# HGRN2 recurrence: value projections computed for two tiles at once, in 512-column products, with the sixteen weight tiles in another order

## The chip, the cores and the metric

The kernel runs on one core of one Trainium2 chip. The metric is the device time of one launch in microseconds. Three runs of the kernel before gave a median of 2646.62 us.

## The reference, cut to what matters

The program is two transformer blocks and a third one with a gated linear recurrence (HGRN2), all on 512 tokens of width 1024, in float32. The change is inside the recurrence stage of the last block. Its input projection gives four tensors, `q`, `f`, `i` (the values, called `v` in the kernel) and `g`:

```python
def _hgrn2_mixer(h, w_in, lower_bound, out_norm, w_out):
    proj = h @ w_in                                  # (512,1024) @ (1024,4096)
    q, f, i, g = jnp.split(proj, 4, axis=-1)
    ...                                              # log_f and k from f, qf = silu(q)/sqrt(128)
    o = _hgrn2_chunk_scan(heads(qf), heads(k), heads(i), heads(log_f))   # 8 heads of 128
    o = o * lax.rsqrt(jnp.mean(o * o, axis=-1, keepdims=True) + NORM_EPS)
    o = o.reshape(b, s, D_MODEL) * out_norm * jax.nn.silu(g)
    return o @ w_out
# S_t = diag(f_t) S_{t-1} + k_t v_t^T ;  o_t = S_t^T q_t
```

## The kernel before

Each float32 product is made of three matmuls on a high and a low part of either operand (hi x hi, hi x lo, lo x hi). The 4096 columns of `hgrn_w_in_2` are taken in sixteen tiles of 1024 x 256, named by tensor and pair of heads: ("f", 0) is the f tile of heads 0 and 1. `HG_TILES` is their order. A tile passes through one of two slots, by its place in the list (even places slot 0, odd places slot 1): SyncE's queue loads it into `w_raw` once the tile two places ahead of it has been split; ScalarE makes `w_hi_t` in two halves (`conv`, line 910) after the last matmul on the tile that held the slot; VectorE makes `w_lo_t` in four quarters (`rest`, line 1207; GpSimd does this in other stages).

A tile is used in two units, and a unit in two fills of one half each (`("gemm", u, h)`). For f, q and g a fill is 12 matmuls with a weight block as the stationary operand and 512 tokens moving (`unit_part`, lines 1785, 1786, 1790). For v the tokens are stationary, 128 at a time, and 256 weight columns move, so that a fill is 24 matmuls (`v_part`, lines 1800 to 1802). ScalarE takes a unit out of its PSUM bank (`unit_out`): two sigmoids for f (lines 850, 851), silu for q and g (853, 858), a scaled copy for v (855) into `hg_v`, which holds one pair of heads.

The order of all steps is written out by `hgrn_sequence`, which every engine walks and from which it picks its own steps. For each pair of heads j = 0..3 there are twelve slots: ten levels of the scan (`lev`: TensorE multiplies keys by queries, VectorE then multiplies Q and K by decay factors, lines 1176 and 1177, in `update`, and keeps the scores in `hg_p`, in `keep`) and two outputs (`out`, line 1723). After the TensorE part of a slot come one or two fills of the projection, which cover VectorE's update for the next level. `after(k, step)` places a step behind the k-th next fill: `prep` (VectorE finishes f and k of a unit, lines 1214 and 1215), `rest`, `far`, and the output norm of the pair before (`hn`, lines 1229 and 1231, and `lo`, line 1236). The order of fills before is v0 f1 q1 g0 in pair 0, v1 f2 q2 g1 in pair 1, v2 f3 q3 g2 in pair 2, v3 g3 in pair 3, with f0 and q0 ahead of the loop; with `HG_FILLS` each of slots 0 to 6 has one fill, slots 7 to 10 have two and slot 11 has one.

VectorE walks its steps in order: a `prep` that waits for ScalarE's sigmoid holds back the `lev` behind it. TensorE waits for `hg_qk` (VectorE's updates) at each level, and for `w_hi` and `w_rest` before the hi and the lo products of a fill on a new tile.

## Time and profile before

| | value |
|---|---|
| median of 3 runs | 2646.62 us |
| lowest, highest | 2646.04, 2647.33 us |
| the profiled execution's own time | 2649.84 us |
| its span in the profile | 2648.0 us |
| TensorE busy | 2593.1 us, 98% of the span |
| granted TensorE clock, mean | 0.992 |
| recurrence, from its first level (1982.56) to the first whole unit of the output projection (2257.70) | 275.1 us |

The profile's clock starts at the first instruction. Starts of matmuls are recorded and their ends are modelled, so a matmul's shown duration is longer than the distance to the next one; distances between starts are what counts. A granted clock of 1.00 is 2.4 GHz, 0.50 is 1.2 GHz, and a value between them is a mean over a stretch that has both.

### The profile page before, as it was taken

What the parts mean: (1) busy time and instruction counts of PE and PEld (TensorE: products, weight loads), DVE (VectorE), ACT (ScalarE), POOL (GpSimd) and SP (SyncE); (2) the same over time, 40 slices, a digit from 0 to 9 for tenths busy, and PEclk for the clock granted to TensorE, in tenths of its full rate; (3) what the DMA queues carried; (4) which work ended last, traced back from release to release, by engine and by line L of the source; (5) the groups of instructions that cost most, each with busy time, mean ns of one, the idle gap of its engine ahead of it and who ended that gap; (6) DMA issues with size and microseconds to landing.
All of it is one profiled execution on the core that took longest, in us unless ns stands there. A gap on an engine that the chain in (4) does not pass through costs nothing.

```text
span 2648.0 us, 30661 instructions
## 1 busy us (share of the span) xinstructions
PE 2593.1 (98%) x12780; PEld 2155.9 (81%) x12780; DVE 1092.8 (41%) x1563; ACT 890.0 (34%) x1361; POOL 1000.3 (38%) x404
## 2 busy tenths in 40 slices
PE   6999999999999999999999999999999999999998
PEld 5788888776888888788888988888888888888887
DVE  5635254454532225844345254211164555512213
ACT  4222225565422223422224333222252333423322
POOL 1445444221454544444444434444430000444442
PEclk8999999999999999999999999999999999999999
DMA  6555344211333343455452324233232221232331
GB/s 242 202 183 199 119 155 130 67 56 48 112 127 127 127 135 124 163 167 183 135 187 88 109 80 163 92 101 100 89 96 64 64 64 49 90 102 96 96 96 64
DMA packets 249088, 310.56 MB, mean 117 GB/s; under 512 B 7356, under 2 KB 228301, under 8 KB 248950
## 3 DMA queue, kind: packets, MB, share of 16 engines
q1 hardware_dynamic: 245962, 304.94, 34.9%
q10 hardware_dynamic: 2988, 3.66, 0.4%
q8 instruction: 101, 1.65, 0.3%
q14 instruction: 37, 0.30, 0.0%
HBM read 306.46 MB, written 4.74 MB: 118 GB/s over the span
## 4 chain that ended last, share of the span: by engine, by line
PE 93%; DVE 3%; DMA 1%; issue 1%; ACT 1%; POOL 0%; SPq 0%; DVEq 0%; ACTq 0%
PE bank L1773 20%; PE bank L1768 20%; PE bank L1769 20%; PE bank L1785 5%; PE bank L1786 5%; PE bank L1790 5%; PE bank L1751 2%; PE bank L1696 2%; PE bank L1752 2%; PE bank L1753 2%; PE bank L1800 1%; PE bank L1801 1%; PE bank L1802 1%; PE bank L1613 1%; PE bank L1633 1%
## 5 line engine op out<-in xcount | busy, mean ns | idle before, releaser
L757 POOL TENSOR_TENSOR w_lo_t<-w_raw,w_hi_t 128x1024 fp32r<-128x1024 f32 (+1 forms) x400 | 1000.1, 2520 | 1617.2 <-ACT w_hi_t L910 1617.0
L910 ACT CAST w_hi_t<-w_raw 128x1024 fp32r<-128x1024 f32 (+1 forms) x432 | 424.9, 1032 | 688.2 <-PE bank L1773 582.6
L1768 PE MATMUL bank<-h_hi,w_hi_t 128*128 128x512 f32 x1648 | 644.4, 391 | 5.2 <-issue 2.7
L1769 PE MATMUL bank<-h_lo,w_hi_t 128*128 128x512 f32 x1648 | 643.2, 390 | 0.0
L1773 PE MATMUL bank<-h_hi,w_lo_t 128*128 128x512 f32 x1648 | 415.2, 391 | 0.0
L1768 PEld LDWEIGHTS bank<-h_hi,w_hi_t 128*128 128x128 f32 x1648 | 310.6, 188 | 71.1 <-issue 3.6
L1769 PEld LDWEIGHTS bank<-h_lo,w_hi_t 128*128 128x128 f32 x1648 | 310.6, 188 | 64.4 <-issue 0.2
L1773 PEld LDWEIGHTS bank<-h_hi,w_lo_t 128*128 128x128 f32 x1648 | 309.3, 188 | 63.9
L1323 DVE SCALAR_TENSOR_TENSOR scr<-scr,cact 128x1024 f32<-128x1024 f32 x112 | 257.7, 2301 | 89.4 <-DMA scr<-in_ada_w 81.2
L1768 PE MATMUL bank<-act_hi,w_hi_t 128*128 128x512 f32 x720 | 280.3, 389 | 1.3 <-ACT w_hi_t L910 1.2
L1769 PE MATMUL bank<-act_lo,w_hi_t 128*128 128x512 f32 x720 | 280.1, 389 | 0.0
L1471 DVE TENSOR_TENSOR bank<-hidden,bank 128x512 f32<-128x512 f32 x88 | 60.9, 694 | 442.1 <-ACT hidden L1050 442.1
L1494 DVE SCALAR_TENSOR_TENSOR x<-bank,half,x 128x512 f32<-128x512 f32 x88 | 66.1, 751 | 338.1 <-PE bank L1773 260.9
L1773 PE MATMUL bank<-act_hi,w_lo_t 128*128 128x512 f32 x720 | 179.0, 389 | 0.4 <-POOL w_lo_t L757 0.4
L1050 ACT ACTIVATE hidden<-bank 128x512 f32<-128x512 f32 x88 | 52.6, 598 | 369.1 <-PE bank L1773 369.1
L1768 PEld LDWEIGHTS bank<-act_hi,w_hi_t 128*128 128x128 f32 x720 | 135.2, 188 | 30.1 <-issue 1.6
L1773 PEld LDWEIGHTS bank<-act_hi,w_lo_t 128*128 128x128 f32 x720 | 135.0, 188 | 29.2 <-POOL w_lo_t L757 1.3
L1769 PEld LDWEIGHTS bank<-act_lo,w_hi_t 128*128 128x128 f32 x720 | 135.2, 188 | 28.0
L1785 PE MATMUL bank<-act_hi,w_hi_t 128*128 128x512 f32 x320 | 129.0, 403 | 3.1 <-DVE act_lo L1147 3.0
L1786 PE MATMUL bank<-act_lo,w_hi_t 128*128 128x512 f32 x320 | 125.4, 392 | 0.0
L1785 PE MATMUL bank<-h_hi,w_hi_t 128*128 128x512 f32 x288 | 121.3, 421 | 0.0
L1790 PE MATMUL bank<-act_hi,w_lo_t 128*128 128x512 f32 x320 | 114.7, 391 | 0.0
(251 smaller groups left out, 3377.4 us busy)
## 6 DMA issues: line engine op xcount, KB each, us to landing
scr<-in_ada_w SPq DMA_DIRECT2D x128, 512.0 KB, 6.8
w_raw<-in_ffn_wg SPq DMA_DIRECT2D x44, 1024.0 KB, 5.3
w_raw<-in_ffn_wu SPq DMA_DIRECT2D x44, 1024.0 KB, 5.4
w_raw<-in_ffn_wd SPq DMA_DIRECT2D x32, 1024.0 KB, 5.3
w_raw<-in_mlp_w SPq DMA_DIRECT2D x32, 1024.0 KB, 5.4
w_raw<-in_hgrn_w_in SPq DMA_DIRECT2D x16, 1024.0 KB, 5.6
w_raw<-in_ffn_wd SPq DMA_DIRECT2D x16, 768.0 KB, 4.7
w_raw<-in_attn_w_qkv SPq DMA_DIRECT2D x12, 1024.0 KB, 5.1
```

Source lines behind the costliest of these rows:

```text
L757: nc.gpsimd.tensor_tensor(w_lo_t[:, t % 2, k], w_raw[:, t % 2, k], w_hi_t[:, t % 2, k].bitcast(F32), ALU.subtract).then_inc(w_lo, 1)
L910: act.copy(w_hi_t[:, slot, k], w_raw[:, slot, k]).then_inc(w_hi, 1)
L1323: dve.scalar_tensor_tensor(acc, src, cact[:, kb:kb + 1], acc, ALU.mult, ALU.add).then_inc(ada_ch, 1)
L1471: dve.tensor_tensor(ps[2 + b][:], blk(hidden, 4 + (2 * i + b) % 4), ps[2 + b][:], ALU.mult).then_inc(v_done, 1)
L1494: ins_ = dve.scalar_tensor_tensor(xb, acc[:], gate_col(op, nb), xb, ALU.mult, ALU.add)
L1696: mm = pe.matmul(ps[2 + s % 2][:, n * 64:(n + 1) * 64], K[:, tok], late, start=True, stop=True)
L1768: pe.matmul(dst, w, blk(m_hi, kb), start=kb == 0, stop=False)
L1769: pe.matmul(dst, w, blk(m_lo, kb), start=False, stop=False)
L1773: last = pe.matmul(dst, w_lo_t[:, slot, kb, b * P:(b + 1) * P], blk(m_hi, kb), start=False, stop=kb == kbs - 1)
L1785: pe.matmul(dst, w, blk(m_hi, kb), start=kb == 0, stop=False)
L1786: pe.matmul(dst, w, blk(m_lo, kb), start=False, stop=False)
L1790: last = pe.matmul(dst, w_lo_t[:, slot, kb, b * P:(b + 1) * P], blk(m_hi, kb), start=False, stop=kb == kbs - 1)
```

## The change

The value tiles are taken in pairs. v0 and v1 are neighbours in the new order (places 2 and 3), v2 and v3 too (places 10 and 11), so that each pair fills both weight slots. A value unit is now one block of 128 tokens for both tiles: its matmuls move 512 weight columns, 256 from each slot, and a fill is 12 matmuls (`v_wide`) where it was 24. `hg_v` has four buffers, and ScalarE's copy is two instructions of 256 columns. Both slots are held until the last unit of the pair, so the `conv` steps of both following tiles stand behind it, one after the other. The order of fills is now v0 v1 f1 q1 | g0 f2 q2 g1 | v2 v3 f3 q3 | g2 g3, in the same slots and counts. The `rest` steps around a value pair, and `hn` and `lo` after pairs 0 and 2, get other places.

```diff
--- before.py
+++ after.py
@@ -267,18 +267,24 @@
 
 
 
-HG_TILES = [("f", 0), ("q", 0), ("v", 0), ("f", 1), ("q", 1), ("g", 0), ("v", 1), ("f", 2), ("q", 2), ("g", 1),
-            ("v", 2), ("f", 3), ("q", 3), ("g", 2), ("v", 3), ("g", 3)]
+HG_TILES = [("f", 0), ("q", 0), ("v", 0), ("v", 1), ("f", 1), ("q", 1), ("g", 0), ("f", 2), ("q", 2), ("g", 1),
+            ("v", 2), ("v", 3), ("f", 3), ("q", 3), ("g", 2), ("g", 3)]
 HG_COL = {"g": 3 * D, "v": 2 * D, "f": D, "q": 0}
 HG_FILLS = (1, 1, 1, 1, 1, 1, 1, 2, 2, 2, 2, 1)
 HG_WO_EARLY = 6
 HG_RESTS = 16
 HG_REST_AT = (2, 3, 3, 4)
+HG_REST_TWO = ((2, 2, 3, 3), (3, 4, 4, 5))
 
 
 def hg_unit(kind, j, b):
 
     return 2 * HG_TILES.index((kind, j)) + b
+
+
+def hg_v_block(u):
+
+    return u - hg_unit("v", HG_TILES[u // 2][1] // 2 * 2, 0)
 
 SG_MIX = {3: (0,), 4: (1, 2), 5: (3, 4), 6: (5, 6), 7: (7,)}
 
@@ -293,9 +299,18 @@
 
     def flush_convs():
         seq.extend(convs)
-        for _, i in convs:
+        for n, (_, i) in enumerate(convs):
             if i < HG_RESTS:
-                for q, k in enumerate(HG_REST_AT):
+                if len(convs) == 2:
+                    places = HG_REST_TWO[n]
+                elif HG_TILES[(i + 2) % 16] in (("v", 1), ("v", 3)):
+                    places = (0, 0, 1, 1)
+                else:
+                    places = HG_REST_AT if i else (1, 2, 2, 3)
+                for q, k in enumerate(places):
+                    if k == 0:
+                        seq.append(("rest", i, q))
+                        continue
                     after(k, ("rest", i, q))
         del convs[:]
 
@@ -303,7 +318,10 @@
         kind, j = HG_TILES[u // 2]
         if kind == "f":
             after(1, ("prep", j, u % 2))
-        if u % 2:
+        if kind == "v":
+            if hg_v_block(u) == TB - 1:
+                convs.extend([("conv", u // 2 - 1), ("conv", u // 2)])
+        elif u % 2:
             convs.append(("conv", u // 2))
 
     def fill(*step):
@@ -348,8 +366,9 @@
                 if j < 3:
                     seq.append(("osum", j))
                     for b in range(2):
-                        after(2 + b, ("hn", j, b))
-                        after(3 + b, ("lo", j, b))
+                        k = 2 + b if j % 2 else 3 + 2 * b
+                        after(k, ("hn", j, b))
+                        after(k + 1, ("lo", j, b))
     fill("wo", 1, 0, 0, HG_WO_EARLY)
     seq.append(("osum", 3))
     fill("wo", 1, 1, 0, HG_WO_EARLY)
@@ -450,7 +469,7 @@
         sg_b = vec[:, V_SG + 8:V_SG + 16]
         sg_wn = hidden[:, 0:1024].rearrange("p (g t) -> p g t", g=8)
         sg_mask = hidden[:, 1024:1152]
-        hg_v = scr[:, 0:1024].rearrange("p (t n) -> p t n", t=TB)
+        hg_v = [scr[:, c:c + 1024].rearrange("p (t n) -> p t n", t=TB) for c in (0, 8640, 9664, 10688)]
         hg_g = scr[:, 1024:2048].rearrange("p (h t) -> p h t", h=2)
         hg_f = scr[:, 2048:4096].rearrange("p (b t) -> p b t", b=2)
         hg_k = scr[:, 4096:6144].rearrange("p (b t) -> p b t", b=2)
@@ -842,8 +861,6 @@
                 act.wait_ge(blk_mm, 2 * op.t0 + u + 1)
                 if kind in "fq" and j >= 2:
                     act.wait_ge(hg_mm, 10 * (j - 1))
-                if kind == "v" and j:
-                    act.wait_ge(o_mm, 8 + 2 * j)
                 if kind == "g" and j:
                     act.wait_ge(o_ok, 8 + 2 * j)
                 if kind == "f":
@@ -852,8 +869,9 @@
                 elif kind == "q":
                     act.activation(hg_q[:, j % 2, cols], bank[:], ACT.Silu).then_inc(hg_ev, 1)
                 elif kind == "v":
-                    act.activation(hg_v[:, 2 * b:2 * b + 2, :], bank[:].rearrange("p (t n) -> p t n", t=2), ACT.Copy,
-                                   scale=H_SCALE).then_inc(hg_ev, 1)
+                    tb, j0 = hg_v_block(u), j // 2 * 2
+                    act.activation(hg_v[j0][:, tb, :], bank[:, 0:TW], ACT.Copy, scale=H_SCALE)
+                    act.activation(hg_v[j0 + 1][:, tb, :], bank[:, TW:2 * TW], ACT.Copy, scale=H_SCALE).then_inc(hg_ev, 1)
                 else:
                     act.activation(hg_g[:, b, :], bank[:], ACT.Silu).then_inc(hg_ev, 1)
 
@@ -1650,7 +1668,7 @@
                     pe.wait_ge(a_lo_s, op.a0 + k1)
                     unit_part(ps[2 * s + b][:], s, b, a_hi_t, a_lo_t, k0, k1, KB)
 
-        def hgrn_pe(pe, op, npre, first, unit_part, v_part, w_half):
+        def hgrn_pe(pe, op, npre, first, unit_part, v_wide, w_half):
             for step in hgrn_sequence():
                 if step[0] == "first":
                     w_half(op.t0, 0)
@@ -1665,9 +1683,8 @@
                             pe.wait_ge(pre_root, npre)
                     bank = ps[u if u < 4 else u % 2]
                     if HG_TILES[u // 2][0] == "v":
-                        if u % 2 == h == 0:
-                            w_half(t, 0)
-                        mm = v_part(bank[:, h * TW:(h + 1) * TW], t % 2, 2 * (u % 2) + h, t if u % 2 == h == 0 else None)
+                        tb = hg_v_block(u)
+                        mm = v_wide(bank[:].rearrange("p (j n) -> p j n", j=2), tb, 4 * h, 4 * h + 4, None if tb else t)
                     else:
                         mm = unit_part(bank[:], t % 2, u % 2, h_hi, h_lo, 4 * h, 4 * h + 4, KB,
                                        t if u % 2 == 0 else None)
@@ -1716,11 +1733,11 @@
                     if b == 0:
                         pe.wait_ge(hg_pc, 9 * (j + 1))
                         pe.wait_ge(hg_far, 3 * j + 3)
-                        pe.wait_ge(hg_ev, hg_unit("v", j, 1) + 1)
+                        pe.wait_ge(hg_ev, hg_unit("v", j | 1, 1) + 1)
                     if j:
                         pe.wait_ge(o_ok, 8 + 2 * (j - 1) + b + 1)
                     for c in range(TB):
-                        mm = pe.matmul(ps[6 - b][:, c * P:S], hg_v[:, c, b * P:(b + 1) * P],
+                        mm = pe.matmul(ps[6 - b][:, c * P:S], hg_v[j][:, c, b * P:(b + 1) * P],
                                        hg_p[:, (b * TB + c) * S:(b * TB + c) * S + S - c * P],
                                        start=c == 0, stop=c == TB - 1)
                     mm.then_inc(o_mm, 1)
@@ -1800,6 +1817,20 @@
                     pe.matmul(dst, h_hi[:, tok], w_hi_t[:, slot, kb, :], start=kb == 0, stop=False)
                     pe.matmul(dst, h_hi[:, tok], w_lo_t[:, slot, kb, :], start=False, stop=False)
                     last = pe.matmul(dst, h_lo[:, tok], w_hi_t[:, slot, kb, :], start=False, stop=kb == KB - 1)
+                return last
+
+            def v_wide(dst, tb, k0, k1, tile):
+
+                toks = [slice(kb * S + tb * P, kb * S + (tb + 1) * P) for kb in range(KB)]
+                if tile is not None:
+                    pe.wait_ge(w_hi, 2 * tile + 2 + k1 // 4)
+                for kb in range(k0, k1):
+                    pe.matmul(dst, h_hi[:, toks[kb]], w_hi_t[:, :, kb, :], start=kb == 0, stop=False)
+                    pe.matmul(dst, h_lo[:, toks[kb]], w_hi_t[:, :, kb, :], start=False, stop=False)
+                if tile is not None:
+                    w_half(tile + 1, k1 // 4 - 1)
+                for kb in range(k0, k1):
+                    last = pe.matmul(dst, h_hi[:, toks[kb]], w_lo_t[:, :, kb, :], start=False, stop=kb == KB - 1)
                 return last
 
             def nat_unit(slot, half_, banks, tile=None):
@@ -2064,7 +2095,7 @@
                                                    sg_v[:, c, g * P:(g + 1) * P], sg_ws[:, g, :], start=True, stop=True)
                                 mm.then_inc(sg_mm, 1)
                 elif op.kind == "hgrn":
-                    hgrn_pe(pe, op, npre, lambda: first_units(op, 0, norm, npre - 1), unit_part, v_part, w_half)
+                    hgrn_pe(pe, op, npre, lambda: first_units(op, 0, norm, npre - 1), unit_part, v_wide, w_half)
 
 INPUTS = [
     "x", "c", "rel_bias", "ada_w", "ada_b", "ln_ffn1", "ffn1_wg", "ffn1_wu", "ffn1_wd", "ln_mix", "ln_ffn2",
```

## Rows read from the trace of the kernel before

**Rows 1.** The page: the span, and the busy time of each engine

```profile
span 2648.0 us, 30661 instructions
PE 2593.1 (98%) x12780; PEld 2155.9 (81%) x12780; DVE 1092.8 (41%) x1563; ACT 890.0 (34%) x1361; POOL 1000.3 (38%) x404
```

**Rows 2.** TensorE's waits, 1982 to 2258: total us, times, longest

```profile
PE bank L1702 <- DVE scr L1177: 1.9, 3, 0.6
PE bank L1696 <- DVE scr L1177: 1.2, 3, 0.4
PE bank L1686 <- ACT scr L853: 0.8, 1, 0.8
```

**Rows 3.** The chain in the recurrence: start us, us, what

```profile
1987.45 1.74 PE bank L1696 x16
...
2001.43 1.73 PE bank L1696 x16
...
2015.06 1.73 PE bank L1696 x16
...
2022.97 1.16 PE bank L1702 x8
...
2065.45 2.00 PE bank L1696 x16
```

**Rows 4.** TensorE's timeline, second to last matmul of a value fill

```profile
1984.54 0.28 PE L1801 MATMUL bank<-w_lo_t,h_hi 128*128 128x256 f32 x1
...
1987.17 0.28 PE L1802 MATMUL bank<-w_hi_t,h_lo 128*128 128x256 f32 x1
```

**Rows 5.** The chain, units of 24 matmuls of 512 columns

```profile
2298.67 1.81 PE bank L1773 x8
...
2325.87 1.81 PE bank L1773 x8
```

**Rows 6.** VectorE's timeline, pair 1, between levels 2 and 3

```profile
2060.91 1.29 DVE L1207 TENSOR_TENSOR w_lo_t<-w_raw,w_hi_t 128x512 fp32r<-128x512 f32 x2
...
2062.72 0.75 DVE L1229 SCALAR_TENSOR_TENSOR sq<-bank,vec,ssq 128x512 f32<-128x512 f32 x1
...
2064.72 0.68 DVE L1177 TENSOR_TENSOR scr<-scr 128x512 f32<-128x512 f32 x1
```

**Rows 7.** ScalarE's timeline at three places

```profile
1965.51 0.37 ACT L965 CAST h_hi<-bank 128x256 fp32r<-128x256 f32 x1 [0.48 <-DVE bank L1298]
1965.78 1.05 ACT L910 CAST w_hi_t<-w_raw 128x1024 fp32r<-128x1024 f32 x1
...
2001.47 0.60 ACT L855 ACTIVATE scr<-bank 128x512 f32<-128x512 f32 x1 [8.72 <-PE bank L1802]
2001.96 1.98 ACT L910 CAST w_hi_t<-w_raw 128x1024 fp32r<-128x1024 f32 x2
...
2019.65 0.60 ACT L850 ACTIVATE scr<-bank 128x512 f32<-128x512 f32 x1 [8.02 <-PE bank L1790]
```

**Rows 8.** The page's DMA issues: count, KB each, us to landing

```profile
w_raw<-in_hgrn_w_in SPq DMA_DIRECT2D x16, 1024.0 KB, 5.6
```

**Rows 9.** TensorE's timeline: the first matmul after a pause, pause in brackets

```profile
444.10 1.10 PE L1602 MATMUL bank<-sq,blk 128*128 128x512 f32 x2 [1.53 <-ACT scr L951]
...
637.63 0.80 PE L1785 MATMUL bank<-act_hi,w_hi_t 128*128 128x512 f32 x1 [3.05 <-DVE act_lo L1147]
...
1117.26 0.50 PE L1768 MATMUL bank<-h_hi,w_hi_t 128*128 128x512 f32 x1 [2.08 <-DVE bank L1471]
...
2635.56 0.70 PE L1826 MATMUL bank<-ssq,ones 128*128 128x256 f32 x2 [1.97 <-DVE ssq L1273]
```

**Rows 10.** Windows: us, busy PE, PEld, DVE, ACT, POOL, PEclk, DMA, GB/s

```profile
442.00:450.00 8.00, 6.47 (x26) 4.59 (x25) 1.50 (x2) 5.02 (x7) 2.40 (x2) 1.00 0.00 0
636.00:644.00 8.00, 6.37 (x18) 4.47 (x19) 3.22 (x13) 2.40 (x9) 0.00 (x0) 0.57 0.04 15
1116.00:1124.00 8.00, 6.75 (x22) 5.37 (x23) 7.72 (x8) 3.07 (x4) 4.56 (x2) 0.79 0.42 146
```

## The prediction

> **What bounds the kernel now.** I read the page first: TensorE is busy 2593.1 of 2648.0 us [rows 1], so time comes only from what TensorE issues or waits for; VectorE at 41% and ScalarE at 34% matter where TensorE waits for them. In the recurrence TensorE's waits add up to 1.9 + 1.2 + 0.8 = 3.9 us in seven pauses [rows 2]. Everything else there is matmuls one behind the other. So the change can give back two things, a shorter value projection and part of 3.9 us, and it can add pauses. A pause costs a little more than it shows, since a 512-column matmul is shown 0.39 us long but the next starts 0.23 us after it: 0.16 us more each.
>
> I then read the chain to price a slot. With a value fill in it, three slots take 2001.43 - 1987.45 = 13.98 us, 4.66 each; with an f fill, three take 2015.06 - 2001.43 = 13.63, 4.54 each [rows 3]. The level's own matmuls are the same in both.
>
> **Term 1, the value products.** There are 16 value fills before and 16 after, all in slots with one fill but the last of each new pair. Before, each has 24 matmuls of 256 columns; after, 12 of 512, which is what an f fill issues. The price of one goes from 4.66 to 4.54, 0.12 us less, so 16 x 0.12 = 1.9 us less. Two bounds. From the distances inside a fill, 22 steps take 1987.17 - 1984.54 = 2.63 us, 0.1195 each [rows 4], and in units of 512 columns five units of 24 take 27.20 us, 0.2267 each [rows 5]: 24 x 0.1195 = 2.87 against 12 x 0.2267 = 2.72, 0.15 a fill and 2.4 us in all. The other bound is 0, if moving two stretches of 256 from two slots costs a restart; I take no such cost, as the f fills too read blocks from different places. I take -1.9, with ends -2.4 and 0.
>
> What fixed part of a matmul is saved can be seen from the same rows: 256 columns at 2.4 GHz are 106.7 ns of the 119.5, and 512 are 213.3 of the 226.7, so about 13 ns of each matmul don't go with its columns, and 192 of these go away. The Trainium skill ("TensorE: Matmul & The Clock Gate", section "Back-to-back issue gap") has the distance as N/2.4 plus 2.5 ns; by that rule the 192 matmuls would give back 0.5 us, and the sum below would be +2.1 instead of +0.7. The rows differ from it, and I go by the rows.
>
> **Term 2, VectorE's late update in pairs 1, 2 and 3.** Three of the pauses are at level 3 of these pairs, 1.2 us in all, 0.4 each [rows 2]. What is late is VectorE's update: between level 2 and the update it does two rests (1.29), `lo`, two `hn` operations, and the second update operation begins at 2064.72 and ends at 2065.40 [rows 6]; TensorE starts at 2065.45 [rows 3]. In pairs 1 and 3 the `lo` is moved behind, and the two rests stay: 0.69 us sooner. TensorE, with three cheaper fills ahead, comes 3 x 0.12 = 0.36 sooner, so a pause of 0.41 becomes about 0.1. In pair 2 the two rests are moved ahead of level 1, but `lo` then waits for ScalarE's copy, which stands behind the value unit's evacuation; I get about the same 0.1. So 3 x 0.3 = 0.9 us less, plus the 0.16 behind each pause where it goes away altogether: I take -1.1, with ends 0 and 3 x 0.57 = -1.7. The steps that are moved later in pairs 1 and 3 (`hn` of the second head at level 4, `lo` at level 5) find VectorE with slack: a slot is 4.54 us and its work there is update 1.3, small products and `keep` about 1.2, norm 1.4. The four quarters of tile 3 that now stand ahead of level 1 in pair 0 end about 0.1 us before that update is wanted; I count 0.
>
> **Term 3, the hand-over after a value pair.** This is the new wait. Before, a tile's `w_hi` was made while TensorE worked on the tile in the other slot. After, both slots are in use up to the last matmul of the pair, and the fill that follows at once, without a level between (slot 7 has two fills), is f1 (or f3) on a tile that isn't converted. Where a value unit ended before a conversion, the last matmul's modelled end was 2001.43 [rows 3], the evacuation started at 2001.47, and the conversion 0.49 later at 2001.96; its first half takes 1.05 [rows 7]. Now the evacuation is two instructions of 256 columns; such an instruction starts the next one 0.27 us later (1965.51 to 1965.78, [rows 7]). So w_hi's first half is there at 0.04 + 2 x 0.27 + 1.05 = 1.63 us after the modelled end, TensorE starts 0.05 later, a pause of 1.68, and with 0.16 the slot loses 1.84. There are two pairs: +3.7 us. Ends: 1.74 each if two copies cost what the one did, 3.5; 2.3 each if they cost 0.49 each and something over, 4.6.
>
> The low part is no further wait: the fill has eight hi products first (8 x 0.2267 = 1.8 us), and VectorE, idle since its update and `keep` of level 7, needs 0.05 and two rests (1.29 us, [rows 6]) from the first half on. The second half of `w_hi` and its rests come a microsecond behind that, ahead of the next fill. Behind the pause on TensorE stand levels 8 and 9, whose updates aren't late. On ScalarE four conversion halves (about 4 us) now stand in one row, and end before the next unit is out. On SyncE's queue the load of g0 (place 6) waits for the rests of f1, some 12 us later than before; it lands in 5.6 us [rows 8], about 6 us before its conversion is due. The load of f2 has more room. No load is added.
>
> **Term 4, `prep`.** Three pauses of 0.64 are at level 8 [rows 2]: sigmoid from 2019.65 [rows 7], then prep, update, level at 2022.97 [rows 3], 3.3 us for what one fill of 2.7 covers. In pairs 0 and 2 the tile f1 or f3 is now one tile later, so this `prep` leaves level 8 and the first `prep` comes ahead of level 9, again with one fill to cover the same chain. The pause goes with it: 0, with ends -1.6 (it vanishes twice) and +1.0 (the rests in front delay it by half a microsecond each).
>
> **The sum.** -1.9 - 1.1 + 3.7 + 0 = +0.7 us. The profiled execution's own time was 2649.84 us (span 2648.0 and 1.8 around it), 3.2 above the median of the runs. I put the sum on the median: 2646.6 + 0.7 = 2647.3 us; the profiled execution would be 2650.5.
>
> **The rivals.**
>
> *Each pause takes the clock down.* The new pauses are longer than any in the recurrence. Elsewhere a pause of 1.53 us was followed by a stretch at 1.00, and pauses of 1.97, 2.08 and 3.05 by falls: 0.79 over the 8 us from 1116, 0.57 over the 8 us from 636 [rows 9, 10]. Mine are about 1.7, between. At 0.79 the 8 us lose 1.7 us, so one fall gives 2649.0 and both give 2650.7, still within 0.2%. The Trainium skill ("TensorE: Matmul & The Clock Gate", section "A second HAM failure mode: psum-queue depth-cycling") warns that small idle times between groups of matmuls make the clock swing; in this trace the seven short pauses of the recurrence didn't, since its clock reads 1.00.
>
> *Slower, outside 0.2%.* The same mechanism at the price of the longest pause: 8 x 0.43 = 3.4 us for each pair, +0.7 + 6.9 = 7.6, 2654.2 us. It decides from two falls of 2.3 us each, that is when TensorE runs at 1.2 GHz for 4.6 us and more after each pause. [...]
>
> *Faster.* The pair's end is cheap (the conversion is quicker than I think), `prep` is covered at level 9, and the fills give the whole 2.4: -2.4 - 1.7 - 1.6 + 3.5 = -2.2, 2644.4. For more than 0.2% both hand-overs would have to be free as well, -5.7.
>
> *It does nothing.* The v fills stay at 4.66 and VectorE stays late: +3.7, 2650.3; still no change that can be told.
>
> **How the numbers follow.** About 0.2% (5.3 us) is what a measurement of this kernel can tell from no change. Sum as forecast, no clock fall: 0.45. One or both pauses with a fall of 1.7 us: 0.32. Nothing gained from the fills or the updates: 0.05. Small gain as in the third rival: 0.10. Dear clock falls or an unseen wait, over 5.3 us: 0.06. Everything covered: 0.02. The range reaches from the small gain, 2644.4, to both falls with some of the ends of term 3, 2651.5. Within 0.2%: 0.45 + 0.32 + 0.05 + 0.10 = 0.92; slower 0.06; faster 0.02.
>
> **What the profile after would show.** Value groups of 128 columns by 512 with 64 instructions for each of three lines, and slots of 4.54 us (term 1; wrong if 4.6 and more). No wait of a level on VectorE over 0.2 us at level 3 (term 2). Two new pauses of TensorE of 1.6 to 1.8 us, put down to ScalarE's conversion (term 3; wrong if rests or loads are named, or if they are much over 2). Pauses of 0.64 at level 9 in pairs 0 and 2, at level 8 in pair 1 only (term 4). A granted clock of 1.00 behind the new pauses; where it is 0.5 for some 3 us, the first rival holds. The forecast fails if the pauses are covered by something that I read as serial, or if a slot after the pair waits again.

## The result, and the profile after

| | before | after |
|---|---|---|
| median, us | 2646.45 (20 runs) | 2651.24 (20 runs) |
| lowest to highest | 2644.27 to 2648.85 | 2647.52 to 2655.03 |
| ratio, with 95% interval | | 1.0020 [1.0014, 1.0026] |
| span of the profiled execution | 2648.0 | 2648.6 |
| recurrence, first level to first whole unit of the output projection | 275.14 | 278.35 |
| from there to the end of the span | 390.3 | 392.5 |

The change made the kernel 4.8 us slower, just inside the 5.3 us that I had called no change; I had forecast 2647.3, 0.7 slower. TensorE issues 12588 matmuls where it issued 12780, so the products were made wide as written. First come TensorE's waits in the recurrence (total us, times, longest), to be held against [rows 2]:

```profile
PE bank L1802 <- ACT w_hi_t L928: 3.5, 2, 1.8
PE bank L1713 <- DVE hidden L1209: 1.3, 2, 1.0
PE bank L1728 <- DVE scr L1195: 1.3, 2, 0.6
PE bank L1703 <- ACT scr L870: 0.8, 1, 0.8
PE bank L1719 <- DVE scr L1195: 0.6, 1, 0.6
```

They are 7.5 us where they were 3.9. The first line is the hand-over after a value pair, which I had forecast (two pauses of 1.8). The second I had not: level 1 (line 1713) waits for VectorE's `keep` (line 1209), 1.0 us in pair 0 and 0.3 in pair 2. Level 3's three pauses of 0.4 are no longer among the waits. The `prep` chain now waits at level 9 twice (1728) and at level 8 once (1719). The chain (start us, us, what) of pair 0 shows the second line at work:

```profile
1978.59 0.97 DVE w_lo_t L1225 x2
1979.56 0.24 issue
1979.80 1.29 DVE w_lo_t L1225 x2
1981.09 1.14 DVE scr L1184
1982.22 1.21 DVE hidden L1209 x2
1983.43 0.14 issue
1983.57 1.97 PE bank L1713 x16
...
1988.36 1.73 PE bank L1713 x16
...
2011.06 1.73 PE bank L1713 x16
...
2020.39 0.89 PE bank L1719 x8
...
2027.37 1.99 PE bank L1728 x8
```

The four quarters of tile v1's split, the update for level 1, and the two parts of `keep` stand one behind the other on VectorE, and level 1 begins when the last is done. From 1988.36 to 2011.06 are five slots of 4.54 us, where value slots took 4.66 [rows 3]. And from level 7 (2011.06) to level 8 (2020.39) are 9.3 us, before 7.9 [rows 3]: the hand-over, against the `prep` pause that has moved to 2027.37. ScalarE's timeline of the hand-over, and TensorE's, to be held against [rows 7]:

```profile
2015.65 0.38 ACT L873 ACTIVATE scr<-bank 128x256 f32<-128x256 f32 x1 [8.45 <-PE bank L1833]
2015.93 0.38 ACT L874 ACTIVATE scr<-bank 128x256 f32<-128x256 f32 x1
2016.20 2.94 ACT L928 CAST w_hi_t<-w_raw 128x1024 fp32r<-128x1024 f32 x3
```

```profile
2017.39 0.47 PE L1802 MATMUL bank<-h_hi,w_hi_t 128*128 128x512 f32 x1 [1.77 <-ACT w_hi_t L928]
```

There are two copies 0.28 apart, then a conversion, for whose first half TensorE waits. The windows of 8 us behind the two pauses, to be held against [rows 10]:

```profile
2016.00:2024.00 8.00, 6.61 (x33) 5.65 (x34) 3.10 (x5) 5.37 (x7) 0.00 (x0) 1.00 0.36 107
2155.00:2163.00 8.00, 6.63 (x33) 5.67 (x34) 3.10 (x5) 5.35 (x7) 0.00 (x0) 1.00 0.39 108
```

The granted clock stayed at 1.00. All this makes +3.2 us for the recurrence. The rest is at the end of the program. These are its last 12 us, in the view of the DMA queues (packets, MB, share of 16 engines):

```profile
q1 hardware_dynamic: 576, 2.10, 43.9%
q8 instruction: 1, 0.02, 1.0%
issues: line engine op xcount, KB each, median us to landing
out<-scr SPq DMA_DIRECT2D x4, 512.0 KB, 5.1
```

In the kernel before, the same view of its last 12 us has no line for the instruction queue, and the four output transfers land in 3.6 us:

```profile
q1 hardware_dynamic: 576, 2.10, 43.9%
issues: line engine op xcount, KB each, median us to landing
out<-scr SPq DMA_DIRECT2D x4, 512.0 KB, 3.6
```

A fetch of 16 KB of instructions now falls among the output transfers. The first of these is issued 383.4 us after the end of the recurrence in either kernel; from there to the end of the span it is 7.0 us before and 9.1 after. SyncE's four issues, before and after:

```profile
2641.08 2.95 SPq L746 DMA_DIRECT2D out<-scr  x4
2639.49 3.88 SPq L765 DMA_DIRECT2D out<-scr  x4
```

The packets in the last 2.0 us of the span, before and after:

```profile
q1 hardware_dynamic: 123, 0.44, 55.5%
q1 hardware_dynamic: 8, 0.03, 3.5%
```

Before, the packets keep coming until shortly before the end. After, nearly all of them are done 2 us before it, and a few of 4 KB follow one at a time.

### The profile page after: what moved, and what is told of

The parts are those of the page before. It is cut to its first block, busy times and chain, and to the rows that moved or that the text cites. A ratio compares the mean times of both kernels' runs of the same rounds, so it can differ in the third digit from the quotient of the medians.

```text
span 2648.6 us, 30275 instructions
## 1 busy us (share of the span) xinstructions
PE 2590.4 (98%) x12588; PEld 2144.4 (81%) x12588; DVE 1092.8 (41%) x1563; ACT 892.1 (34%) x1370; POOL 997.4 (38%) x404
## 4 chain that ended last, share of the span: by engine, by line
PE 93%; DVE 3%; ACT 1%; DMA 1%; issue 1%; POOL 0%; SPq 0%; DVEq 0%; ACTq 0%
PE bank L1790 20%; PE bank L1785 20%; PE bank L1786 20%; PE bank L1802 5%; PE bank L1803 5%; PE bank L1807 5%; PE bank L1768 2%; PE bank L1713 2%; PE bank L1769 2%; PE bank L1770 2%; PE bank L1631 1%; PE bank L1651 1%; PE bank L1817 1%; PE bank L1740 1%; PE bank L1818 1%
```

## The experiments

Each is compared with the kernel before, executed beside it on the same chip; the median of that was 2646.6 beside r1 to r4, 2646.7 beside r5 to r8, 2647.0 beside r9 to r12 and 2646.6 beside r13 to r16. Times are in us; "to the end" is from the end of the recurrence to the end of the span. Both stretches are read from the one profiled execution of each run.

| run | recurrence | to the end | median | ratio, 95% interval |
|---|---|---|---|---|
| r1 changed, again | 278.35 | 392.1 | 2651.90 | 1.0022 [1.0013, 1.0030] |
| r2 rests later | 276.82 | 392.1 | 2650.57 | 1.0018 [1.0009, 1.0027] |
| r3 level 8 first | 276.57 | 392.5 | 2649.78 | 1.0015 [1.0006, 1.0024] |
| r4 narrow products | 279.73 | 390.5 | 2652.25 | 1.0023 [1.0014, 1.0033] |
| r5 before, again | 275.13 | 390.3 | 2647.14 | 1.0000 [0.9991, 1.0009] |
| r6 convert first | 277.24 | 392.0 | 2649.34 | 1.0014 [1.0005, 1.0022] |
| r7 longer pause | 286.82 | 392.6 | 2661.13 | 1.0050 [1.0038, 1.0063] |
| r8 three mended | 273.92 | 392.3 | 2647.40 | 1.0002 [0.9993, 1.0011] |
| r9 changed, padded | 278.32 | 390.3 | 2656.41 | 1.0034 [1.0022, 1.0047] |
| r10 before, padded | 275.16 | 390.3 | 2656.22 | 1.0033 [1.0020, 1.0045] |
| r11 mended, padded | 273.93 | 390.7 | 2653.03 | 1.0025 [1.0016, 1.0034] |
| r12 chain covered, padded | 271.16 | 390.7 | 2651.06 | 1.0014 [1.0005, 1.0023] |
| r13 changed, light pad | 278.31 | 390.3 | 2649.54 | 1.0010 [1.0001, 1.0019] |
| r14 chain covered | 271.08 | 392.2 | 2644.89 | 0.9996 [0.9987, 1.0004] |
| r15 chain covered, light pad | 271.15 | 390.7 | 2642.59 | 0.9986 [0.9977, 0.9995] |
| r16 before, fills shared out | 272.37 | 390.3 | 2642.92 | 0.9987 [0.9978, 0.9996] |

**The changed kernel once more** (no edit).

> The changed kernel once more, unaltered. The profile of the changed kernel shows the recurrence 278.35 us long (before: 275.14), +3.2 us, while the medians of 20 runs each differ by 4.8. Theory A: the whole effect is the +3.2 us of the recurrence; the other 1.6 are places outside it that come out differently from run to run; then this profile again shows 278.3 to 278.5 us there and a clock of 1.00 behind the two new pauses, and the ratio may lie anywhere from 1.000 to 1.003. Theory B: in some executions the new pauses of 1.77 us take the clock to 1.2 GHz; then, if this profile catches one, the 8 us behind a pause read 0.79 and the stage is 280 us or more.

The recurrence repeats to a hundredth of a microsecond, and the clock was 1.00 behind both pauses again. That bears out theory A for the recurrence. But the ratio came out at 1.0022, and the end took 392.1 us again, so the rest is no chance either.

**The two quarters behind level 1.**

```diff
                 elif HG_TILES[(i + 2) % 16] in (("v", 1), ("v", 3)):
-                    places = (0, 0, 1, 1)
+                    places = (0, 0, 2, 2)
```

> One edit to the changed kernel: the last two quarters of the split of tiles v1 and v3 stand behind level 1 on VectorE and not ahead of it. Theory A (the two quarters ahead of level 1 delay VectorE's update and its keep of level 0, for which TensorE waits at level 1): the pause of 1.01 us at level 1 of pair 0 goes, that slot's fill goes from 4.02 to about 2.9 us, and in pair 2 from 3.32 to about 2.9; the recurrence becomes 1.5 us shorter, 276.8. Rival (that pause has another cause, such as the wait on ScalarE's conversion of v1): both stay, 278.3.

276.82 against 276.8 expected. The wait for `keep` is no longer among TensorE's waits:

```profile
PE bank L1802 <- ACT w_hi_t L928: 3.5, 2, 1.8
PE bank L1728 <- DVE scr L1195: 1.3, 2, 0.6
PE bank L1703 <- ACT scr L870: 0.8, 1, 0.8
PE bank L1719 <- DVE scr L1195: 0.6, 1, 0.6
```

So the two moved quarters had cost 1.53 us, 1.10 in pair 0 and the rest in pair 2.

**Level 8 ahead of the first f fill.**

```diff
-            counts = HG_FILLS
+            counts = HG_FILLS if j == 1 else (1, 1, 1, 1, 1, 1, 1, 1, 3, 2, 2, 1)
```

(Pair 3 keeps its own counts.)

> One edit to the changed kernel: in pairs 0 and 2 slot 7 has one fill and slot 8 three, so that level 8 stands between the last value fill and the first f fill. Theory A (the pause is the fixed time from the last value matmul to the first half of the converted tile): level 8's 0.8 to 0.9 us now cover part of it, the pause falls from 1.77 to about 0.9 in both pairs, and the recurrence becomes 1.7 us shorter, 276.6, if VectorE's update for level 8 is in time (it has one fill of 2.84 us for 1.4). Rival (TensorE only changes what it waits for, since level 8 then waits for its update or level 9's chain starts as late as now): the gain is under 0.5 us.

276.57, as expected. The hand-over's two pauses are 0.88 each, and of TensorE's other waits none has grown:

```profile
PE bank L1802 <- ACT w_hi_t L928: 1.8, 2, 0.9
PE bank L1713 <- DVE hidden L1209: 1.3, 2, 1.0
PE bank L1728 <- DVE scr L1195: 1.3, 2, 0.6
```

**Narrow products in the new order.** Each value fill computes one tile for one block of tokens. The name `v_wide` here stands for the argument of `hgrn_pe`, which gets `v_part` in this run (last two lines):

```diff
-                        mm = v_wide(bank[:].rearrange("p (j n) -> p j n", j=2), tb, 4 * h, 4 * h + 4, None if tb else t)
+                        if tb == 0:
+                            w_half(t + h, 0)
+                        mm = v_wide(bank[:, h * TW:(h + 1) * TW], h, tb, None if tb else t + h)
...
-                    hgrn_pe(pe, op, npre, lambda: first_units(op, 0, norm, npre - 1), unit_part, v_wide, w_half)
+                    hgrn_pe(pe, op, npre, lambda: first_units(op, 0, norm, npre - 1), unit_part, v_part, w_half)
```

> One edit to the changed kernel: new order and four buffers, but each value fill is again 24 matmuls of 256 columns (all of one tile for a block of 128 tokens, fill 0 from v0 or v2, fill 1 from v1 or v3). It separates the width from the order. Theory A (a fill of 24 costs 2.95 us to the next level and one of 12 costs 2.84): 16 fills are 0.11 dearer, the recurrence is 1.8 us longer than the changed kernel's 278.35, 280.1. Rival 1 (bound of the forecast, distances inside a fill): 2.4 us longer, 280.8. Rival 2 (by the Trainium skill, page TensorE: Matmul & The Clock Gate, section Back-to-back issue gap, 2.5 ns of fixed cost for each of 192 matmuls): 0.5 us longer, 278.9.

279.73: the wide products are worth 1.4 us here, less than my 1.9. A part of the difference is that the first fill of pair 0 ends in the wait for `keep` in either form (4.02 us from its start to level 1 with 24 matmuls and with 12). To the end it took 390.5 us, about as the kernel before, though the order is the new one; it has TensorE's instruction count of the kernel before.

**The kernel before once more** (no edit).

> The kernel before, unaltered. The changed kernel's recurrence took 278.35 us in both profiles and the kernel before's 275.14 in the one there is; the medians differ by 5, so some 1.8 us are not in the recurrence. The profiled execution of before was 3.2 us slower than its own median. Theory A: the recurrence takes 275.1 again, and what lies outside it differs between executions by 1 to 3 us at the same few places in both kernels (around 39, 145, 649 and 1162 us, and behind the last matmul). Theory B: outside the recurrence the kernel before is always quicker by 1 to 2 us, at one place that can be named, and this profile shows it. The ratio is 1.000 within 0.001.

275.13, and 390.3 to the end again. Theory B is right, and its place is the end: in the profiles so far, kernels with wide products took 392.1 to 392.5 us there, the kernel before and the one with narrow products 390.3 to 390.5. What differs ahead of the recurrence comes in steps of 1.3 to 1.9 us at 100, 640 and 1120 us, where the granted clock is or isn't low for a while; this happens between two executions of the same kernel too. At the pause of 2.08 us of [rows 9], 8 of the 18 profiles of this document show such a low stretch behind it and 10 don't, and r5 is one of the 10 although the first profile of the same kernel [rows 10] has it. So a median hangs on how often such falls come, besides the stage that is changed.

**The conversion's first half ahead of the evacuation.** In `hgrn_act`, for the last unit of a pair:

```diff
+                    if HG_TILES[u // 2] in (("v", 1), ("v", 3)) and u % 2:
+                        t = op.t0 + u // 2 + 1
+                        act.wait_ge(blk_mm, 2 * op.t0 + u + 1)
+                        conv_half(t % 2, t, 0)
                     unit_out(u)
```

(`u` is the unit; the `conv` step that comes later then makes the second half alone.)

> One edit to the changed kernel: on ScalarE the first half of the conversion of f1 and f3 stands ahead of the evacuation of the last value unit, and no longer behind it. Theory A (the pause is 0.04 + two evacuations + 1.05 + 0.05): it falls by the two evacuations' 0.54, from 1.77 to 1.23, in both pairs; recurrence 278.35 - 1.1 = 277.3. Rival (the evacuation isn't on that path, since the pause is set by VectorE's split or the landing of the tile): no change, 278.3.

277.24: the pauses are 1.23 each, where 1.77 - 0.54 = 1.23 was expected. So the two copies are on the path, as I had said.

**A longer pause.**

```diff
                     act.activation(hg_v[j0 + 1][:, tb, :], bank[:, TW:2 * TW], ACT.Copy, scale=H_SCALE).then_inc(hg_ev, 1)
+                    if j % 2 and tb == TB - 1:
+                        act.preload_act_table(ACT.Sigmoid)
```

> One edit to the changed kernel: ScalarE loads its sigmoid table (1.28 us) between the last value unit's evacuation and the conversion, and not after it, so that each hand-over pause is 3.05 us where it was 1.77. Theory A: pauses of 1.97 us and more were followed by a stretch at 1.2 GHz, so the windows of 8 us behind these two read 0.8 or less, and the recurrence gets longer by 2 x 1.28 and by 1.7 us or more for each fall: 284 us or more. Rival: the clock doesn't fall behind these pauses, and the recurrence is 278.35 + 2.6 = 280.9.

The loading of a table stands between the copies and the conversion. The pauses were 3.19 and 3.20 us, and in both windows of 8 us behind them TensorE ran at 1.2 GHz most of the time:

```profile
2020.00:2028.00 8.00, 6.97 (x23) 5.77 (x24) 3.10 (x5) 3.72 (x4) 0.00 (x0) 0.57 0.39 121
2163.00:2171.00 8.00, 6.82 (x22) 5.66 (x23) 3.10 (x5) 3.88 (x4) 0.00 (x0) 0.57 0.41 116
```

Of the 8.5 us that the recurrence got longer, 2.8 are the pauses, so a fall cost 2.8 us. That is less than the 3.4 at which the prediction priced a window of 0.57 [rows 10], and more than the 1.7 for the window behind the 2.08 us pause.

**Three edits together** (those of r2, r3 and r6).

> The three edits together (last two quarters of v1's and v3's split behind level 1; level 8 ahead of the first f fill in pairs 0 and 2; first half of the conversion ahead of the evacuation). If the three costs are separate they add: 278.35 - 1.5 - 1.8 - 1.1 = 273.9 us for the recurrence, 1.2 below the kernel before's 275.14. Rival (they overlap, because the pause behind the pair then waits on VectorE's split or level 9's chain sets the end): 275 us or more. In the medians, 2646 to 2648 us: the 1.8 us that lie outside the recurrence should stay.

273.92: they add up. Yet the median is that of the kernel before within its interval, not 1.2 below it, and the end took 392.3 us.

**Padding, heavy.** If the fetch in the output transfers is what takes 2 us, it should move when instructions are added in front:

```diff
+            for _ in range(32):
+                pe.matmul(ps[1][:, 0:1], ident[:], ident[:, 0:1], start=True, stop=True)
             pe.wait_ge(init_a, 1)
             first_ada(0)
```

> In every profile of the changed order with wide products an instruction fetch (queue q8, 16 KB) falls into the last 12 us, among the four output transfers, and the time behind the last matmul is 6.1 to 7.6 us; in both profiles of the kernel before, and in the one with narrow products, there is no such fetch and it is 5.35 to 5.41. The change takes 384 instructions off TensorE. Here 32 one-column float32 matmuls (128 instructions of matmul and weight load) are added to the changed kernel while TensorE waits at the start, so that the instruction count behind them sits where the kernel before's does, counted in chunks of 256. Theory A (the place of the fetch is set by the instruction count): no fetch at the end, 5.4 us behind the last matmul, recurrence unchanged at 278.35, and the median falls by about 1.8 to 2650. Rival (the fetch there has another cause, or it isn't what costs the time): it stays, as do 7 us and a median of 2651.5.

> The same 128 instructions added to the kernel before, which puts its count where the changed kernel's is. Theory A: the fetch now falls into the output transfers, the time behind the last matmul goes from 5.35 to 6.1 to 7.6 us, the recurrence stays at 275.13, and the median rises by 1.5 to 2 us, to 2648.3. Rival: nothing changes but noise, 2646.6.

> The three mends of the run before together with the 128 instructions. If recurrence and end are separate they add: recurrence 273.92, 5.4 us behind the last matmul, median 2646.66 - 1.2 = 2645.4, ratio 0.9995. Rival (the padding costs time at the start, or the fetch moves to another costly place): 2647 or more.

The padding itself took 13.8 us at the start, where 4.3 were idle, so these medians say nothing of the end. The profiles do: in r9 there is no fetch in the last 12 us and the end takes 390.3 us instead of 392.5, in r11 390.7 instead of 392.3. But r10 missed: with the same padding the kernel before has no fetch at the end either, and 390.3. The trace narrows that down. The last three fetches of queue q8 stand 77.1, 47.1 and 22.7 us ahead of the end in the kernel before, and 91.6, 62.2 and 34.2 in r10, so the padding moved them earlier by 12 to 15 us. In the changed kernel they stand at 64.6, 35.8 and 8.1; the one that would correspond to the last of these is missing in r10. So the remainder of the count (in chunks of 256 instructions, about what TensorE starts between two fetches) shifts the fetches, but doesn't say which one is the last. r10 has the remainder of the changed kernel and 512 instructions of TensorE more.

**The sigmoid chain covered**, on top of the three edits:

```diff
-            counts = HG_FILLS if j == 1 else (1, 1, 1, 1, 1, 1, 1, 1, 3, 2, 2, 1)
+            counts = (1, 1, 1, 1, 1, 1, 1, 1, 3, 2, 2, 1) if j == 1 else (1, 1, 1, 1, 1, 1, 1, 1, 4, 2, 1, 1)
```

> As the mended and padded kernel, and the fills of slots 7 to 11 are shared out so that two fills, not one, lie between the unit whose sigmoid VectorE must finish and the level behind it: 1, 4, 2, 1, 1 in pairs 0 and 2, and 1, 3, 2, 2, 1 in pair 1. Theory: the three pauses of 0.64 us, the chain sigmoid, prep, update, go (0.8 each with the modelled end), recurrence 273.92 - 2.4 = 271.5, median 2643. Rival (the outputs, with one fill behind the first of them, now wait for ScalarE's copies, or level 8 for its update): 273 or more.

271.16: all three pauses of 0.64 are gone, and with them 2.8 us, 0.9 for each.

**A light padding.** The same 32 one-column matmuls in bf16 are 64 instructions and took 1.0 us of the idle start:

> The changed kernel with 64 instructions more at TensorE's idle start: 32 one-column bf16 matmuls, which should fit into the 4.3 us of waiting there (the 128 of the runs before took 13.8 us and put 3 to 6 us in front of everything). By TensorE's rate near the end (256 instructions in about 29 us) the last instruction fetch moves from 6 to 8 us ahead of the end to about 14 to 15, ahead of the output transfers. Theory A: from the end of the recurrence to the end of the span 390.3 us, where the changed kernel has 392.5 and 392.1 and the kernel before 390.3 twice; recurrence 278.35; median 2651.6 - 2 = 2649.7, ratio 1.0012. Rival (what matters is something else in those 128 instructions, or 64 are too few): 392 us there.

The median is 2649.5, 2.9 above the kernel before beside it, where the changed kernel without padding was 4.8 and 5.3 (r1) above. The end went from 392.1 to 390.3 us, with the recurrence as it was. The last 12 us have only the output transfers again:

```profile
q1 hardware_dynamic: 576, 2.10, 43.9%
issues: line engine op xcount, KB each, median us to landing
out<-scr SPq DMA_DIRECT2D x4, 512.0 KB, 3.6
```

**The chain covered, without padding and with the light one** (the five edits together are those of r2, r3 and r6, the covered chain, and the light padding).

> The mended kernel with the covered sigmoid chain (recurrence 271.16 in its padded form), without any padding. Theory A: recurrence 271.2, then 392.3 us with the fetch in the output transfers, median 2646.7 - 4.0 + 2.0 = 2644.7, ratio 0.9992. Rival (the sigmoid chain's gain was bound to the padded start): recurrence near 273.9.

> The same with the light padding of 64 instructions. Theory A: recurrence 271.2, then 390.3 us, no fetch in the last 12 us, median 2646.7 - 4.0 = 2642.7, ratio 0.9985, the fastest so far. Rival: the padding gives nothing, 2644.7, or costs time at the start, 2645 and more.

2644.89 and 2642.59: 2.3 us between a kernel with the fetch there and one without. The two differ in the padding alone.

**The kernel before with only its fills shared out.**

```diff
-            counts = HG_FILLS
+            counts = (1, 1, 1, 1, 1, 1, 1, 1, 3, 2, 2, 1)
```

> The kernel before with only the fills of slots 7 to 11 shared out as 1, 3, 2, 2, 1, so that level 8 stands ahead of the first fill of the next tile and two fills lie between the unit whose sigmoid is waited for and level 9. It asks how much of the best version's gain has nothing to do with the value pairs. Theory: the three pauses of 0.64 us at level 8 go, recurrence 275.13 - 2.4 = 272.7, end unchanged at 390.3, median 2644.2, ratio 0.9991. Rival (level 8 now waits for its own update, with one fill of 2.84 over it): 274.5 or more.

The recurrence is 2.8 us shorter and the median 2642.92, which is 3.7 below the kernel before; 0.9 of that is more than the recurrence shows, and the ratio's interval is wide enough for it. One line in the kernel before does as much for the time as the value pairs with all five edits (2642.59; the intervals lie over one another). The pairs' own recurrence is 1.2 us shorter still (271.15), and their end 0.4 longer (390.7). TensorE's waits that are left in r16, and in r15:

```profile
PE bank L1696 <- DVE scr L1177: 1.2, 3, 0.4
PE bank L1686 <- ACT scr L853: 0.8, 1, 0.8
```

```profile
PE bank L1712 <- ACT scr L871: 0.8, 1, 0.8
PE bank L1811 <- ACT w_hi_t L937: 0.7, 2, 0.3
```

## Why the prediction was wrong

The forecast of +0.7 us was short by 4. Two things were missing, one in the recurrence and one outside it, and two terms were a little off in size.

*Term 2, its last sentence.* The step that failed is "The four quarters of tile 3 that now stand ahead of level 1 in pair 0 end about 0.1 us before that update is wanted; I count 0." Two things in it were wrong. The quarters did not end in time: on VectorE they ended 1.1 us after the moment at which the update could start, as r2 shows, where the update begins 2.13 us behind the start of the first level and not 3.23. The update itself still came in time (it ended at 1982.22, and TensorE was ready at 1982.56). But level 1 also waits for `keep` of level 0, which VectorE does behind the update: `pe.wait_ge(hg_pc, 9 * j + max(2, s))` asks for it at s = 1. It ended at 1983.43, and I had not counted it. Pair 2 has the same, which I passed over. r2 measured both together: 1.53 us.

*Nothing in the sum for the end of the program.* I counted fewer matmuls as time only. They are also 384 instructions fewer (matmuls and weight loads), and with that count a 16 KB instruction fetch falls among the last four transfers: from the end of the recurrence on, the eight profiles that have it there took 392.0 to 392.6 us and the ten that haven't 390.3 to 390.7. The difference lies behind the issue of the first output transfer, from which it is 8.4 to 9.1 us to the end in the eight and 6.9 to 7.0 in the ten. r13 took the fetch away and 1.9 to 2.4 us of the median with it (its 2.9 above the kernel before against 4.8 and 5.3); r14 and r15 differ in nothing but the padding and are 2.3 apart. No run moved the fetch without changing the instruction count; that it costs the time itself is read from the transfers behind it.

The other steps held in their mechanism.

*Term 1.* Slots of 4.54 us, as forecast. r4 prices the width at 1.4 us, where I had 1.9. The bound of 2.4, from the distances within a fill, was too high: 13 ns is what those distances show, but not all of it comes back. A fill of 24 takes 2.94 to 2.96 us to the next level and one of 12 takes 2.82 to 2.86, about 0.1 us for twelve matmuls, and fills that end in a wait give nothing. The Trainium skill's formula of N/2.4 + 2.5 ns ("TensorE: Matmul & The Clock Gate", section "Back-to-back issue gap") would have made it an estimated 0.5 us; the run lies between. The section gives that formula for a single matmul by itself; for a stream of weight loads and matmuls it gives 131 ns at 512 columns, where the distance in this kernel is 226.7 [rows 5].

*Term 2, level 3.* The waits of 0.4 fell to under 0.1, as forecast. From level 0 to level 4 pairs 1 and 3 take 0.73 us less than before, and pair 0, which never had that pause, 0.30 less once `keep` is out of the way (r2), so a level 3 gave 0.43. With pair 2 (0.65 less in r2) the three gave 1.2, for my 1.1.

*Term 3.* Two pauses of 1.77 us, 1.68 forecast. The 0.09 is the step from the end of the converted half (2017.25) to TensorE's start (2017.39), 0.14 where I had 0.05. r6 and r3 took the pause apart: 0.54 of it is the evacuation, and 0.89 can be covered by level 8. A slip in the range: with its own numbers the cheap end of a pair is 0.04 + 0.49 + 1.05 + 0.05 + 0.16 = 1.79, not 1.74.

*Term 4.* The `prep` pauses of pairs 0 and 2 moved to level 9 and are as long as they were, 0.64; pair 1's stayed at level 8.

The sum with what was measured: from level 7 to level 8 the changed kernel takes 9.33 us, the kernel before 7.91 [rows 3] with 0.64 of `prep` pause in it that is only moved, so a hand-over cost 9.33 - 7.27 = 2.06, not 1.84, and two cost 4.1. With -1.4 for the width, -1.2 at level 3 and +1.5 for `keep` that makes +3.0; the recurrence showed +3.2. With 2 us at the end it is +5.2, and the medians say +4.8 and, for r1, +5.3 (2651.90 against 2646.61 beside it).

*Luck.* The profiled execution took 2650.40 us, and I had forecast 2650.5. That is luck: the profiled execution of the kernel before was 3.2 above its median and this one 0.8 below. It is luck too that 2651.24 lies under the upper end of my range, 2651.5: that end stood for two falls of the clock, and there was none in the recurrence.

*The rivals.* "Each pause takes the clock down" did not happen: the granted clock was 1.00 behind all twelve pauses of 1.77 in the six profiles that have them (the changed kernel's, r1, r2, r4, r9 and r13). r7 shows that the mechanism is real: both of its pauses of 3.2 us were followed by a fall. What [rows 9, 10] show for the 2.08 us pause is one outcome of two, 8 falls in 18 profiles. "Slower, outside 0.2%" put the loss at the clock, in the wrong place. The Trainium skill's warning of a swinging clock ("TensorE: Matmul & The Clock Gate", section "A second HAM failure mode: psum-queue depth-cycling") didn't hold for these pauses, with 1.00 in both windows.

*What stays open.* Which fetch is the last one: the padding moved it in the changed kernel as reckoned, and in the kernel before it moved the earlier ones, but none came behind them (r10). And how a fetch of 16 KB holds up four transfers of 512 KB was not tried. The trace shows that the fetch itself took 1.95 us in the changed kernel (0.9 to 1.8 in the other seven), that SyncE's third issue took 1.90 us where it takes 0.33 in the kernel before (it is as long in six of the eight), and that the last packets came one at a time; that they are the share of the output which stood behind the fetch is my reading and not shown.

## What to carry to other kernels

Here, taking both buffers of a double-buffered operand for one wide product saved a tenth of a microsecond a fill and cost a hand-over of about two: price the first use after the pair before the products in it. When a step is put ahead of another on an engine, check every wait for what that engine does next, not only for its first result; here it was the second result, `keep`, that was late. Where the profile shows a pause of a dependence chain, look first at whether the existing fills can be shared out differently: here one line gave as much as the whole redesign. And look at the end of the program too when a change removes instructions elsewhere.

## What the runs showed of the hardware that I had not expected

An instruction fetch (one transfer of 16 KB on queue q8) that falls among the last output transfers comes with a median time to land of 4.4 to 5.1 us in eight profiles, where it is 3.1 to 3.6 in the ten without, and the end comes 1.4 to 2.2 us later, counted from the first output transfer; its place changes with the number of instructions ahead of it (r9, r13). A pause of TensorE of 1.77 us left the clock at 2.4 GHz twelve times out of twelve, and the two of 3.2 us in r7 were followed by 0.57 over 8 us. In between it came out either way: the same pause of 2.08 us [rows 9] was followed by a low stretch in 8 profiles and by none in 10. One-column float32 matmuls at the program's start took 13.8 us for 64 in the trace (0.22 each), and 32 in bf16 took 1.0 (r9, r13).
